# GpSimd's 31 convolution sums dealt anew over the projection chunks of a layer

## The chip, the cores and the metric
The kernel runs on one core of one Trainium2 chip. The metric is the device time of an execution in microseconds (us); the number compared is the median of the runs.

## The reference
A first block (pooling, sparse attention, convolutional feed-forward) is followed by a second block of two layers, in float32, for 512 tokens of width 1024. The change lies in the mixing layer of the second block, which both layers run:

```
u = h @ w_in
a_b, a_c, a_x, q, k, v, c_in = split(u)
y_a = a_b * causal_depthwise_conv(a_c * a_x, short_conv_w)          # 3 taps
o   = rmsnorm(diff_attention(rope(q), rope(k), v, lam)) * (1 - lam_init)   # 4 heads
c   = c_in + glu_b
c   = c[:, :256] * sigmoid(c[:, 256:])
c   = causal_depthwise_conv(c, conf_dw_w) + conf_dw_b               # 31 taps, 256 channels
y_c = silu(layernorm(c))
out = concat(y_a, o, y_c) @ w_out
```
The 31-tap convolution is `conv[t] = b + sum over k of w[k] * c[t - 30 + k]`, for each of 256 channels. They lie as two groups of 128 on the partitions.

## The kernel before
Activations are kept transposed, features on the partitions and the 512 tokens along the free axis. A product with weights runs through chunks. A chunk is eight 128x128 weight blocks (512 KB), 1024 input by 128 output features, and gives one 128x512 output tile (in a group of four chunks the blocks are dealt otherwise). To keep float32 accuracy with the faster float32r matmuls, every operand is split in a high part and a remainder: `wh` and `wl` for the weights, `xh` and `xl` for the activations. A chunk is 24 matmuls: per block `wh*xh` and `wh*xl` (16, L486 and L487, or L543, L544, L574, L575 in grouped chunks), then eight `wl*xh` (L506, L550, L582).

The chunks go through the engines like this:
- SyncE loads chunk t into one of four slots of `raw`. It waits until the remainder of chunk t-4 is done.
- ScalarE makes the high part: `head(t)`, a copy `wh <- raw` (L972, 128x1024). There are two slots, so head(t+2) waits until TensorE has finished chunk t.
- GpSimd makes the remainder: `rest(t)`, two subtractions `wl <- raw, wh` (L428), after head(t). Here it is called a pass.
- TensorE waits for `hi_ready` before the first matmul of a chunk and for `lo_ready` before the last eight.
- VectorE takes the result out of PSUM.

The projection of a layer of the second block has 22 chunks (n = 0 to 21). Chunks 0 to 3 compute the 31-tap convolution's input together (a group over four banks), 4 to 7 the values, 8 to 15 the queries and keys of four heads in turn, 16 to 21 the three-tap branch. The order on every engine is written out by hand. Beside chunk n each engine has two slots, s = 2n and 2n + 1. From slot 21 on the attention steps of head h occupy slots 21 + 4h to 31 + 4h: scores (TensorE, L892 and L894), maximum (VectorE, L1823), exponentials (ScalarE, L1229), scaling of the probabilities (VectorE, L1832 and L1328), transposes (TensorE, L904), the product with the values (TensorE, L911), and the norm.

The queries and keys need a rotation. When chunk n (8 to 15) is done, ScalarE copies the bank to `ybuf` (L972, `rope_in`) and then does head(n + 2). TensorE rotates it in the first slot of chunk n + 1 (L881), VectorE multiplies and adds (L1331 or L1900; L1789; L1793 writes `lq` or `lk`). The score of a head's first step waits for the rotated key.

The 31-tap convolution is dealt between the engines. VectorE does channel group 0: one fused multiply and add per tap (L1328, `conv <- cpad, par, conv`), 23 of them up to the first slot of chunk 10 and then one per chunk. Group 1 is done by two engines. ScalarE writes the product of tap k, `tprod <- cpad` (L972, in the function `products` of the scalar block), and GpSimd adds it: `tap(k)`, a drain (L446), a wait for the product (L447) and `conv <- conv, tprod` (L448); tap 0 is a multiply on GpSimd itself (L443). Two product buffers alternate, so the product of tap k waits for the sum of tap k - 2 (`tap_added`). Tap 0 and the products wait for `glu_out`, VectorE's signal that the convolution's input is there (L1813).

GpSimd's order before is: pass of chunk n, then from chunk 5 on some sums: three each in chunks 5 to 9 (15), two each in 10 to 17 (16). ScalarE's order within chunk n is, for each of the two slots: the attention steps, then products; at the end the wait for TensorE's chunk n, the ybuf copy, head(n + 2), and for n = 7 the four copies of the values. It makes 2 and 1 products in the two slots of chunks 5 to 9 and 1 and 1 after.

The sums' result is read for the layer norm in slot 38 (chunk 19).

Of the kernel before, what the change touches and what calls it, by code (L numbers as in the profile page):

```python
# [46 lines left out]
TAPS = 31  # L47
# [42 lines left out]


HEAD_SLOT = 21

Y_ORDER = ("head0", "head1", "ya0", "head2", "head3", "ya1", "conv0", "conv1")
NORM_OF_HEAD = (1, 2, 3, 5)
# [34 lines left out]
def layer_slots(n):  # L130

    for half in range(2):
        s = 2 * n + half
        yield s, [(h, s - HEAD_SLOT - 4 * h) for h in range(4) if 0 <= s - HEAD_SLOT - 4 * h <= 10]

# [7 lines left out]
def build(nc, x, positions, positions2, weights, par1, par2, consts, masks, w1, w2, pool_w, out):  # L143
    ctx = ExitStack()
    with ctx:
# [65 lines left out]
        def c2(name, i=0):  # L211
            return par[:, P2[name] + i:P2[name] + i + 1]
# [133 lines left out]
        def cols(start, n):  # L346
            return slice(start, start + n) if isinstance(start, int) else bass.ds(start, n)
# [71 lines left out]
        @block.gpsimd  # L419
        def _(pool):  # L420
            def rest(t):

                v = t.value()
                pool.wait_ge(hi_ready, (t + 1).value())
                half = CB * P // 2
                for h in range(2):
                    two = cols((v % 2) * (CB * P) + h * half, half)
                    x_ = pool.tensor_tensor(wl[:, :, :].rearrange("p s n -> p (s n)")[:, two],  # L428
                                            raw[:, cols((v % 4) * (CB * P) + h * half, half)],
                                            wh[:, :, :].rearrange("p s n -> p (s n)")[:, two].bitcast(F32),  # L430
                                            ALU.subtract)
                x_.then_inc(lo_ready, 1)

            with pool.Fori(0, T_BLOCK1) as t:
                rest(Count(0).loop(t, 1))

            with pool.Fori(0, LAYERS) as l:
                T = Count(T_BLOCK1).loop(l, T_LAYER)

                def tap(k):  # L440

                    if k == 0:
                        pool.tensor_scalar(conv[:, 1, :], cpad[:, 1, 0:S], c2("dw_w", TAPS), c2("dw_b", 1),  # L443
                                           ALU.mult, ALU.add)
                    else:
                        pool.drain()  # L446
                        pool.wait_ge(R["tap_prod"], Count(k).loop(l, TAPS - 1).value())  # L447
                        pool.tensor_tensor(conv[:, 1, :], conv[:, 1, :], tprod[:, k % 2, :], ALU.add)\  # L448
                            .then_inc(R["tap_added"], 1)

                done = 0
                for n in range(T_LIN):
                    if n == 5:
                        pool.wait_ge(R["glu_out"], Count(1).loop(l, 1).value())
                    rest(T + n)
                    if n >= 5:
                        upto = min(done + (3 if n < 10 else 2), TAPS)
                        for k in range(done, upto):
                            tap(k)
                        done = upto  # L460
                with pool.Fori(T_LIN, T_LAYER) as t:
                    rest(T.loop(t, 1))
            for t in range(T_ALL, T_ALL + 2):
                rest(Count(t))
# [505 lines left out]
        def _(act):  # L970
            def copy(o, i, scale=1.0):
                return act.activation(o, i, ACT.Copy, scale=scale)  # L972
# [140 lines left out]
            for p in range(NP):  # L1113
                j, k = p // 8, p % 8
                t, n = T_IN + 3 * j, N_IN + 4 * j
# [25 lines left out]
            for j in range(NT):  # L1141
                t, n = T_IN + 12 + 3 * j, N_IN + 16 + 4 * j
# [6 lines left out]
                for c in range(2):  # L1149
                    k = 2 * j + c  # L1150
# [3 lines left out]
            def out_and_ffn(t, n, u, feed0, gain, h0, first_block):  # L1154
                def next_head(c):
                    act.wait_ge(chunk_done, (t + (c + 1)).value())
                    head(t + (c + 2))

                for c in range(4):
                    next_head(c)  # L1160
                for m in range(KD):
                    if m >= 4:
                        next_head(m)
                    feed(m, feed0 + m, gain("ffn_g", m), n + m)
                t, n = t + T_OUT, n + KD
                for c in range(2):
                    next_head(c)
                root(u, NT, scale=1.0 / D)
                for c in range(2, 4):
                    next_head(c)  # L1170
                hidden(n, h0, 0, first_block)
                next_head(4)
                hidden(n + 2, h0 + 1, 1, first_block)
                next_head(5)
                hidden(n + 4, h0 + 2, 2, first_block)
                with act.Fori(3, KF) as r:
                    for c in range(2):
                        act.wait_ge(chunk_done, (t + (c + 1)).loop(r, 2).value())
                        head((t + (c + 2)).loop(r, 2))
                    hidden(n.loop(r, 2), h0.loop(r, 1), r, first_block)  # L1180
                return t + T_UP, n + T_UP
# [27 lines left out]
            t, n = out_and_ffn(Count(T_IN + T_MIX), Count(N_IN + N_MIX), Count(8), Count(KD), gain1, Count(0), True)  # L1209
# [3 lines left out]
            with act.Fori(0, LAYERS) as l:  # L1213
# [24 lines left out]
                def y_head(name, src):  # L1238
                    copy(yh[:, Y_ORDER.index(name), :], src).then_inc(R["y_hi"], 1)
# [27 lines left out]
                def products(n):  # L1267

                    for k in range(made[0], min(made[0] + n, TAPS)):
                        if k == 1:  # L1270
                            act.wait_ge(R["glu_out"], L1.value())
                        if k > 2:
                            act.wait_ge(R["tap_added"], Count(k - 2).loop(l, TAPS - 1).value())
                        copy(tprod[:, k % 2, :], cpad[:, 1, k:k + S], scale=c2("dw_w", TAPS + k))\
                            .then_inc(R["tap_prod"], 1)
                    made[0] += n

                for n in range(4, T_LIN):
                    for half, (s, steps) in enumerate(layer_slots(n)):
                        if s == 11:  # L1280
                            act.wait_ge(R["lam_psum"], L1.value())
                            act.activation(lame, TR[:, 0:2], ACT.Exp).then_inc(R["lam_exp"], 1)
                        if s == 38:
                            act.wait_ge(R["ya_ready"], Count(1).loop(l, 2).value())
                            y_head("ya0", ya[:, 0, :])
                        for h, step in steps:
                            head_step(h, step)
                        if n >= 5:
                            products(2 if n < 10 and half == 0 else 1)
                        if s == 38:  # L1290
                            root(U0 + NORM_LN[0], NT, scale=1.0 / 256, plain=True)
                        if s == 40:
                            act.wait_ge(R["ln_sub"], L1.value())
                            act.activation(sq[:, :, :], conv[:, :, :], ACT.Square).then_inc(R["ln_sq"], 1)
                        if s == 42:
                            root(U0 + NORM_LN[1], NT, scale=1.0 / 256, eps=LN_EPS)
                    act.wait_ge(chunk_done, (T + (n + 1)).value())
                    if 8 <= n < 16:
                        i, m = n - 8, n - 4
                        if i >= 2:  # L1300
                            act.wait_ge(rot_ready, Count(6 + i).loop(l, 8).value())
                        b = QK0[i] if i < 2 else G[(N + m).even()]
                        copy(ybuf[:, i % 2, :], b[:, :]).then_inc(R["rope_in"], 1)
                    head(T + (n + 2))
                    if n == 7:
                        act.wait_ge(recip_ready, (U0 + 1).value())
                        for i in range(NT):
                            copy(lv[:, :, i, :], VB[i][:, :].rearrange("p (h d) -> p h d", d=P),
                                 scale=s_recip[:, i:i + 1]).then_inc(R["v_out"], 1)
                act.wait_ge(R["ya_ready"], Count(2).loop(l, 2).value())  # L1310
                y_head("ya1", ya[:, 1, :])
                for c in range(2):
# [4 lines left out]
                t, n = out_and_ffn(T + T_LIN, N + N_LIN, U0 + 7, Count(3 * KD).loop(l, 2 * KD), gain2,  # L1317
                                   Count(KF).loop(l, KF), False)
# [776 lines left out]
```

## Time and profile before

| | |
|---|---|
| median of 3 runs | 1987.17 us (1985.21 to 1987.58) |
| profiled execution: time, span | 1989.08 us, 1987.3 us |
| TensorE busy, mean granted clock | 1918.2 us (97%), 0.987 |
| VectorE, ScalarE, GpSimd busy | 964.4, 735.3, 970.4 us |
| projection stage of layer 0, of layer 1 | 764 to 957, 1368 to 1559 us |

The profile comes from one execution; its times are measured from the start of the span. PE is TensorE, PEld its weight loads, DVE VectorE, ACT ScalarE, POOL GpSimd, and POOLq is GpSimd's sequencer (drains and waits). L446 is line 446 of the kernel. In a time line, what stands in brackets is how long the engine sat idle before the instruction and what released it. Matmuls overlap, so eight in a row take less than eight times one.

### The profile page before, as it was taken

Reading aid. Unit: us, or ns where it says so; the run is one execution under the profiler, and the core shown is the slowest. Engines: PE = TensorE matmul, PEld = TensorE weight load, DVE = VectorE, ACT = ScalarE, POOL = GpSimd, SP = SyncE. Lnnn points to the kernel's source line nnn. Section 1 sums busy time; section 2 is a strip of 40 time slices with the busy share of each in tenths; the row PEclk is TensorE's granted clock in tenths of the full one; section 3 lists DMA queues with packets and bytes.
Section 4 is the critical chain, followed back from the end, with each engine's and each line's share of the span. In section 5 each row is a group of like instructions: output and inputs, shape, how many; then the busy total and the mean of one; then the engine's idle time right before and its main releaser. Section 6 shows DMA issues by size and latency. Waiting matters only on the chain.

```text
span 1987.3 us, 28229 instructions
## 1 busy us (share of the span) xinstructions
PE 1918.2 (97%) x8670; PEld 1515.1 (76%) x8670; DVE 964.4 (49%) x1316; ACT 735.3 (37%) x1160; POOL 970.4 (49%) x692
## 2 busy tenths in 40 slices
PE   6999999999999999899999999999899999999996
PEld 5866668878888888667788888887666788888885
DVE  7667644456665122877443333221977443333213
ACT  4235553432223223455433322222555443332222
POOL 4322224446666454853444555454854345455553
PEclk9999999999999999999999999999999999999998
DMA  6111112222222322211232222232111222322232
GB/s 242 64 54 43 44 54 95 96 85 95 95 95 95 106 99 92 73 45 54 79 101 96 95 95 95 98 103 98 63 54 61 77 90 92 104 95 95 95 106 84
DMA packets 48952, 173.89 MB, mean 88 GB/s; under 512 B 5488, under 2 KB 6512, under 8 KB 48624
## 3 DMA queue, kind: packets, MB, share of 16 engines
q1 hardware_dynamic: 48880, 172.96, 25.8%
q8 instruction: 42, 0.69, 0.1%
q14 instruction: 30, 0.25, 0.0%
HBM read 169.82 MB, written 2.10 MB: 87 GB/s over the span
## 4 chain that ended last, share of the span: by engine, by line
PE 81%; DVE 6%; POOLq 3%; issue 3%; DVEq 2%; ACT 2%; POOL 1%; DMA 1%; ACTq 0%; SPq 0%
PE bank L506 21%; PE bank L486 20%; PE bank L487 20%; PE bank L543 3%; PE bank L550 3%; PE bank L544 3%; POOLq L446 3%; PE bank L520 1%; PE bank L744 1%; PE bank L526 1%; PE bank L521 1%; DVE lp L1832 1%; PE bank L773 1%; POOL wl L428 1%; PE bank L787 1%
## 5 line engine op out<-in xcount | busy, mean ns | idle before, releaser
L428 POOL TENSOR_TENSOR wl<-raw,wh (+1 forms) x626 | 883.6, 1433 | 921.7 <-ACT wh L972 907.9
L972 ACT ACTIVATE wh<-raw 128x1024 fp32r (+1 forms) x313 | 331.7, 1060 | 827.1 <-PE bank L506 694.4
L486 PE MATMUL bank<-xh,wh 128*128 128x512 f32 x1336 | 533.2, 399 | 5.5 <-DVE tmp L1371 5.5
L487 PE MATMUL bank<-xl,wh 128*128 128x512 f32 x1336 | 524.3, 392 | 0.0
L506 PE MATMUL bank<-xh,wl 128*128 128x512 f32 x1336 | 343.2, 396 | 3.4 <-POOL wl L428 3.4
L486 PEld LDWEIGHTS bank<-xh,wh 128*128 128x128 f32 x1336 | 253.7, 190 | 65.5 <-issue 7.9
L506 PEld LDWEIGHTS bank<-xh,wl 128*128 128x128 f32 x1336 | 249.6, 189 | 63.8 <-issue 7.1
L487 PEld LDWEIGHTS bank<-xl,wh 128*128 128x128 f32 x1336 | 253.5, 190 | 56.4 <-issue 3.8
L486 PE MATMUL bank<-hh,wh 128*128 128x512 f32 x528 | 208.0, 394 | 0.0
L487 PE MATMUL bank<-hl,wh 128*128 128x512 f32 x528 | 208.0, 394 | 0.0
L1371 DVE TENSOR_TENSOR ybuf<-bank,rstd 128x512 f32<-128x512 f32 x95 | 65.3, 688 | 227.2 <-PE bank L506 225.2
L1740 DVE TENSOR_TENSOR tmp<-tmp,ybuf 128x512 f32<-128x512 f32 x66 | 106.6, 1614 | 74.4 <-ACT tmp L1189 74.2
L1702 DVE TENSOR_TENSOR xs<-xs,bank 128x512 f32<-128x512 f32 (+1 forms) x48 | 32.1, 684 | 227.7 <-PE bank L506 179.3
L506 PE MATMUL bank<-hh,wl 128*128 128x512 f32 x528 | 134.8, 394 | 0.0
L448 POOL TENSOR_TENSOR conv<-conv,tprod 128x512 f32<-128x512 f32 x60 | 85.4, 1424 | 80.7 <-ACT tprod L972 72.6
L506 PEld LDWEIGHTS bank<-hh,wl 128*128 128x128 f32 x528 | 98.7, 187 | 24.5
L486 PEld LDWEIGHTS bank<-hh,wh 128*128 128x128 f32 x528 | 98.7, 187 | 24.4
L487 PEld LDWEIGHTS bank<-hl,wh 128*128 128x128 f32 x528 | 98.7, 187 | 24.4
L543 PE MATMUL bank<-xh,wh 128*128 128x512 f32 x192 | 76.8, 400 | 9.1 <-ACT wh L972 8.4
L972 ACT ACTIVATE hh<-tmp 128x512 f32 (+1 forms) x66 | 41.7, 632 | 117.1 <-DVE tmp L1740 117.1
L1328 DVE SCALAR_TENSOR_TENSOR conv<-cpad,par,conv 128x512 f32<-128x512 f32 x60 | 80.4, 1340 | 4.9
L1742 DVE TENSOR_TENSOR hl<-tmp,hh 128x512 f32 (+1 forms) x66 | 51.1, 774 | 59.8 <-ACT hh L972 59.8
(285 smaller groups left out, 2333.0 us busy)
## 6 DMA issues: line engine op xcount, KB each, us to landing
raw<-in_weights SPq DMA_DIRECT2D x313, 512.0 KB, 3.2
xs<-in_x SPq DMA_DIRECT2D x4, 512.0 KB, 6.9
out_t<-xs SPq DMA_DIRECT2D x8, 256.0 KB, 2.2
w1k<-in_w SPq DMA_DIRECT2D x1, 1024.0 KB, 9.6
w1v<-in_w SPq DMA_DIRECT2D x1, 1024.0 KB, 11.1
shifted<-kvraw SPq DMA_DIRECT2D x8, 124.0 KB, 2.4
posi<-in_positions SPq DMA_DIRECT2D x2, 256.0 KB, 8.8
cst<-in_consts SPq DMA_DIRECT2D x1, 290.0 KB, 5.4
```

Of the source, the lines that this page charges most:

```text
L428: x_ = pool.tensor_tensor(wl[:, :, :].rearrange("p s n -> p (s n)")[:, two], raw[:, cols((v % 4) * (CB * P) + h * half, half)], wh[:, :, : ...
L446: pool.drain()
L448: pool.tensor_tensor(conv[:, 1, :], conv[:, 1, :], tprod[:, k % 2, :], ALU.add)\
L486: mm(b[:, :], w, kh(k), start=first and k == 0, stop=False)
L487: mm(b[:, :], w, kl(k), start=False, stop=False)
L506: i = mm(b[:, :], wl[:, s, (blk0 + k) * P:(blk0 + k + 1) * P], kh(k), start=False, stop=last and k == blocks - 1)
L543: mm(X4[a][:, :], w, kh(k), start=k == 0, stop=False)
L544: mm(X4[a][:, :], w, kl(k), start=False, stop=False)
L972: return act.activation(o, i, ACT.Copy, scale=scale)
L1328: return stt(out=o, in0=a, scalar=s, in1=b, op0=ALU.mult, op1=ALU.add)
L1371: return tt(o, b[:, :], rstd[:, :], ALU.mult).then_inc(tile_out, 1)
L1740: tt(tmp[:, 1, :], tmp[:, 0, :], ybuf[:, 0, :], ALU.mult).then_inc(R["prod_ready"], 1)
```

## The change
GpSimd's sums follow a table: none in chunk 5, three in 6, two in 7, four in each of 8 to 13, two in 14. The wait for `glu_out` on GpSimd moves from ahead of pass 5 to ahead of pass 6. ScalarE's products follow the same table, one chunk ahead: in each of the two slots of chunk n it makes half (rounded down) of the sums that GpSimd has in chunk n + 1. Those are 1 and 1 in chunks 5 and 6, 2 and 2 in 7 to 12, 1 and 1 in 13, none after. Operations, data and their number are the same.

```diff
--- before.py
+++ after.py
@@ -90,6 +90,8 @@
 
 
 HEAD_SLOT = 21
+
+POOL_TAPS = {6: 3, 7: 2, 8: 4, 9: 4, 10: 4, 11: 4, 12: 4, 13: 4, 14: 2}
 
 Y_ORDER = ("head0", "head1", "ya0", "head2", "head3", "ya1", "conv0", "conv1")
 NORM_OF_HEAD = (1, 2, 3, 5)
@@ -450,14 +452,13 @@
 
                 done = 0
                 for n in range(T_LIN):
-                    if n == 5:
+                    if n == 6:
                         pool.wait_ge(R["glu_out"], Count(1).loop(l, 1).value())
                     rest(T + n)
-                    if n >= 5:
-                        upto = min(done + (3 if n < 10 else 2), TAPS)
-                        for k in range(done, upto):
-                            tap(k)
-                        done = upto
+                    for k in range(done, done + POOL_TAPS.get(n, 0)):
+                        tap(k)
+                    done += POOL_TAPS.get(n, 0)
+                assert done == TAPS
                 with pool.Fori(T_LIN, T_LAYER) as t:
                     rest(T.loop(t, 1))
             for t in range(T_ALL, T_ALL + 2):
@@ -1285,8 +1286,7 @@
                             y_head("ya0", ya[:, 0, :])
                         for h, step in steps:
                             head_step(h, step)
-                        if n >= 5:
-                            products(2 if n < 10 and half == 0 else 1)
+                        products(POOL_TAPS.get(n + 1, 0) // 2 if n >= 5 else 0)
                         if s == 38:
                             root(U0 + NORM_LN[0], NT, scale=1.0 / 256, plain=True)
                         if s == 40:
```

## Rows read from the trace of the kernel before
**Rows 1.** The page's first part: busy us, share, instructions of each engine.
```profile
PE 1918.2 (97%) x8670; PEld 1515.1 (76%) x8670; DVE 964.4 (49%) x1316; ACT 735.3 (37%) x1160; POOL 970.4 (49%) x692
```
**Rows 2.** The chain of waits, 800 to 836 us: shares of the stretch by line.
```profile
by line: POOLq L446 70.8%; POOL wl L428 22.1%; issue 8.1%; POOL conv L448 1.5%; POOLq L447 1.1%; POOLq L428 0.6%; POOLq L424 0.4%
```
**Rows 3.** Time line of GpSimd: start, us, engine, line, operation, out<-in, [idle before <-releaser].
```profile
792.62 2.74 POOL L428 TENSOR_TENSOR wl<-raw,wh 128x512 fp32r<-128x512 f32 x2 [6.80 <-DVE cpad L1813]
799.90 3.41 POOL L428 TENSOR_TENSOR wl<-raw,wh 128x512 fp32r<-128x512 f32 x2
...
819.69 1.47 POOL L448 TENSOR_TENSOR conv<-conv,tprod 128x512 f32<-128x512 f32 x1 [0.23 <-issue]
821.39 1.48 POOL L448 TENSOR_TENSOR conv<-conv,tprod 128x512 f32<-128x512 f32 x1 [0.23 <-issue]
...
832.99 3.43 POOL L428 TENSOR_TENSOR wl<-raw,wh 128x512 fp32r<-128x512 f32 x2
...
851.68 1.28 POOL L448 TENSOR_TENSOR conv<-conv,tprod 128x512 f32<-128x512 f32 x1 [2.71 <-ACT tprod L972]
```
**Rows 4.** Waits of TensorE, 760 to 1000 us: us in total, times, longest.
```profile
PE bank L892 <- DVE lk L1793: 5.0, 3, 2.3
PE bank L582 <- POOL wl L428: 4.3, 2, 2.8
PE bank L506 <- POOL wl L428: 1.6, 2, 0.8
PE bank L881 <- ACT ybuf L972: 1.0, 2, 0.8
```
**Rows 5.** Time line of TensorE, layer 0.
```profile
811.98 3.78 PE L582 MATMUL bank<-wl,xh 128*128 128x512 f32 x8 [2.83 <-POOL wl L428]
...
820.42 1.98 PE L506 MATMUL bank<-xh,wl 128*128 128x512 f32 x8
...
837.51 0.29 PE L892 MATMUL bank<-msk 128*128 128x128 bf16 x2
```
**Rows 6.** Windows: length, busy us (count) of PE, PEld, DVE, ACT, POOL; PEclk; DMA; GB/s.
```profile
799.90:836.65 36.75, 30.07 (x111) 22.00 (x110) 35.09 (x27) 16.32 (x24) 33.49 (x24) 0.91 0.17 58
810.00:820.00 10.00, 8.02 (x23) 6.34 (x24) 9.63 (x7) 5.39 (x8) 9.10 (x8) 0.66 0.15 52
880.00:890.00 10.00, 8.54 (x36) 6.20 (x37) 7.59 (x15) 5.47 (x14) 6.18 (x4) 0.83 0.16 54
```
**Rows 7.** Time line of ScalarE, layer 0: head, product, rotation copies.
```profile
792.89 1.06 ACT L972 ACTIVATE wh<-raw 128x1024 fp32r x1 [1.39 <-PE bank L582]
...
822.90 0.73 ACT L972 ACTIVATE tprod<-cpad,par 128x512 f32<-128x512 f32 x1 [0.98 <-POOL conv L448]
823.53 0.58 ACT L972 ACTIVATE ybuf<-bank 128x512 f32<-128x512 f32 x1
...
832.02 0.58 ACT L972 ACTIVATE ybuf<-bank 128x512 f32<-128x512 f32 x1
...
839.89 0.59 ACT L972 ACTIVATE ybuf<-bank 128x512 f32<-128x512 f32 x1
...
885.98 0.59 ACT L972 ACTIVATE ybuf<-bank 128x512 f32<-128x512 f32 x1
```
**Rows 8.** Time line of VectorE, layer 0.
```profile
818.30 6.80 DVE L1328 SCALAR_TENSOR_TENSOR conv<-cpad,par,conv 128x512 f32<-128x512 f32 x4
...
835.98 0.99 DVE L1793 TENSOR_TENSOR lk<-tmp,tmp 128x512 f32<-128x512 f32 x1
...
882.82 1.61 DVE L1328 SCALAR_TENSOR_TENSOR lp<-lp,small 128x512 f32<-128x512 f32 x1
...
930.40 0.75 DVE L1328 SCALAR_TENSOR_TENSOR lp<-lp,small 128x512 f32<-128x512 f32 x1
```
**Rows 9.** Time line of ScalarE, layer 1: head 6 and chunk 10's copy.
```profile
1396.65 1.07 ACT L972 ACTIVATE wh<-raw 128x1024 fp32r x1 [1.39 <-PE bank L582]
...
1443.51 0.59 ACT L972 ACTIVATE ybuf<-bank 128x512 f32<-128x512 f32 x1
```

## The prediction
> **What bounds the kernel now.** I began with the page. TensorE is busy 97% of the span [rows 1], so only stretches in which it waits or runs slowly can be won, and only new ones can be lost. GpSimd is at 49%, but that is an average. In the two layers' projection stages the chain of waits is different: from 800 to 836 us, 70.8% of it is GpSimd's drain (L446) and 22.1% the remainder pass (L428) [rows 2]. So I went through the engines' time lines there. "Chunk n" is projection chunk n (0 to 21) of layer 0; ACT is ScalarE, DVE is VectorE.
>
> GpSimd does one remainder pass per chunk, then its sums. Pass 6 starts at 799.90, pass 7 at 808.55 and pass 10 at 832.99: (832.99 - 799.90)/4 = 8.27 us per chunk of one pass and three sums. Sums follow each other every 1.70 us (819.69, 821.39). So a pass with its gaps is 8.27 - 5.10 = 3.17 us [rows 3]. TensorE needs less for a chunk (24 matmuls, eight of them in 1.98 us [rows 5]), and waits for passes 6, 7, 9 and 10, 4.3 + 1.6 = 5.9 us in four waits [rows 4]. After the longest, 2.83 us, its granted clock is 0.66 over 810 to 820 [rows 6]: between 1.2 and 2.4 GHz that is 6.8 us at the lower level, 3.4 us of work lost (eight matmuls take 3.78 us there [rows 5]). That is about 9 us per layer on TensorE's side.
>
> ACT is tied to the same chain. Product k waits for sum k-2 (two buffers). At the end of chunk n, behind that chunk's products in ACT's order, come the copy of the rotation input (ybuf) and head n+2. The ybuf copy of chunk 8 starts at 823.53, 0.63 us after a product that had waited 0.98 us for GpSimd; that of chunk 9 at 832.02, that of chunk 10 at 839.89 [rows 7]. TensorE's rotation waits up to 0.8 us for them [rows 4].
>
> DVE has no slack either: 35.09 us busy of 36.75 from 799.90 to 836.65, its own sums at 1.70 us, in step with GpSimd's (four in 6.80) [rows 6, 8]. It finishes the first rotated key at 835.98 + 0.99 = 836.97 [rows 8]; TensorE takes it at 837.51 [rows 5]. So whatever happens to the remainder waits, the first score cannot come over 0.5 us earlier unless DVE is faster, and it does the same operations beside a GpSimd that is still busy.
>
> **The change part by part.**
>
> *Wait for glu_out one pass later.* Pass 5 no longer waits 6.80 us [rows 3]. It moves from 792.62 to about 789. TensorE waited only for the four passes above, so this gains nothing there; it only takes one pass out of the queue behind the wait. GpSimd's chain now begins with pass 6, which needs head 6: ACT ends that at 792.89 + 1.06 = 793.95 [rows 7]. The old chain began at 792.62.
>
> *Sums and products.* Before, sums per GpSimd chunk: 3 in chunks 5 to 9, 2 in 10 to 17. After: 3 in 6, 2 in 7, 4 in 8 to 13, 2 in 14. ACT's products by chunk were 3 in 5 to 9, then 2; now 2 in 5 and 6, 4 in 7 to 12, 2 in 13. The last product of ACT's chunk n used to need the second sum (chunks 10 up: the first) of GpSimd's chunk n. Now, in chunks 7 to 12, it needs the second sum of GpSimd's chunk **n+1**, behind pass n+1. Behind it on ACT stand ybuf and head n+2, for which TensorE, DVE and GpSimd wait.
>
> I follow GpSimd with the measured pieces. The first cycle (pass and sums 0 to 2) takes 799.90 - 792.62 = 7.28. Then a pass is 3.17 and a sum 1.70.
> Pass 7 starts at 793.95 + 7.28 = 801.2; pass 8 at + 6.57 (two sums) = 807.8; pass 9 at + 9.97 (four sums) = 817.8; pass 10 at 827.7; pass 11 at 837.7.
> The second sum of a chunk ends 3.17 + 3.40 = 6.57 after its pass starts: sum 6 at 814.4, sum 10 at 824.3, sum 14 at 834.3, sum 18 at 844.3.
> A product's 0.63 us later ybuf starts: at 825.0 for chunk 8 (before 823.53, +1.5), 835.0 for chunk 9 (before 832.02, +3.0), 844.9 for chunk 10 (before 839.89, +5.0).
> GpSimd has no gap in this: a product is there 0.7 us after the sum two before it, and a head ends 1.6 us after the start of the ybuf copy ahead of it (0.58 and 1.06): head 10 at 826.6 for the pass at 827.7, head 11 at 836.6 for 837.7.
>
> The last piece is uncertain: DVE's dense sums end near 836, and beyond that a sum takes 1.28 (at 851.68) instead of 1.47 (at 819.69) [rows 3]. Passes took between 2.74 and 3.43 [rows 3]; I take 0.4 less there. That makes +5.0 into +4.2. I take +4.7 for a layer at the chunk-10 copy. TensorE's four remainder waits go, but it waits instead for head 9 and for the copies of chunks 8 and 9 (some 6 to 8 us for the first: it would arrive near 818), so the 9 us do not come back. Such a wait is longer than the one that was followed by the lower clock; that slow stretch would end before the next copy, so I add nothing.
>
> Layer 1 repeats this: from head 6 to the copy of chunk 10 it has 1443.51 - 1396.65 = 46.86 us [rows 9], layer 0 has 47.00. So +9.4 us for the early term.
>
> The Trainium skill ("SBUF — State Buffer", section "Who interferes with whom") says that a VectorE operation with two SBUF inputs and a GpSimd operation that reads SBUF exclude each other for the whole instruction. Taken strictly, a pair would cost 1.28 + 0.75 = 2.03 us, and the cycle of four sums 11.3 us, which would put the chunk-10 copy another 6 us later in each layer (18 sums at 0.33). The trace has 1.70 for a pair [rows 3, 8], so the slowing is there but not the full exclusion; the sum above goes by 1.70.
>
> *After chunk 10.* Here GpSimd keeps up (four sums and a pass in 9.97 against (885.98 - 839.89)/4 = 11.5 us for a chunk [rows 7]), and the chain runs through DVE, ACT and TensorE: the score maximum, the exponentials, the product, ybuf, then DVE's multiply of it and the scaling of the probabilities. In either kernel 13 or 14 of GpSimd's sums are left for this part. Differences:
> - ACT: one more product between exponentials and ybuf in chunks 11 and 12, +0.63 each by [rows 7]; one less in 14, 15 and 16, -0.63 each.
> - DVE: the same operation on the probabilities takes 1.61 beside GpSimd and 0.75 alone [rows 8]. The sums are denser in chunks 11 to 13 and gone in 15 to 17. A second sum right behind the first in chunks 10 to 12 falls on DVE's scaling of the probabilities: two operations of that kind, up to +1.7 a chunk. From 14 on about 0.9, one such, comes back a chunk.
> - What can come back on TensorE: its three waits for the rotated keys, 5.0 us in all, 2.3 the longest [rows 4], and slow clock behind them (0.83 over 880 to 890 [rows 6]: 1.7 us of work).
>
> Bounds for this term in a layer: -7 (5.0 + 1.7, all of it goes) and +6 (three chunks at +1.7, two products at 0.63). I take 0, since the same number of sums meets the same chain. Both layers: -14 to +12.
>
> The end of the sums (chunk 14 instead of 17) is worth nothing by itself: the layer norm that needs them is in slot 38 (chunk 19).
>
> **Sum.** Early +9.4 (8.4 to 10.2), late 0 (-14 to +12): the profiled execution, 1989.08 us (span 1987.3 and 1.8 around it), becomes 1998.5. It lay 1.9 above the median 1987.17; against that median the forecast is 1996.6.
>
> **The rivals.**
> 1. *Slower by contention too* (chance 0.2): the late term near its upper end, where GpSimd's second sum keeps falling on DVE's scaling and slow stretches follow longer waits. 1987.2 + 9.4 + 9 = 2006. For it: 1.61 against 0.75. Against: GpSimd idles more from chunk 15 on.
> 2. *Made good later* (0.15): TensorE's waits in chunks 14 to 16 are shorter by what the products and sums no longer take, 4 to 5 us a layer, 9 in all. 1987.2 + 9.4 - 9 = 1988: no change.
> 3. *Faster* (0.15), the other side: the copies of chunks 8 to 10 turn out not to hold TensorE, because GpSimd's pieces are quicker once its order is less tight, and the remainder waits with their slow clock (9 us a layer) are gained. Its point of decision is whether sum 10 ends before about 821 (instead of 824.3), and DVE must speed up too. At half its worth, 1987.2 - 9 = 1978. Against it: DVE's 836.97.
> 4. The forecast (0.5): 1997, own range 1992 to 2002.
>
> That the sums would not move at all is excluded by the code.
>
> **How the numbers follow.** Two in ten outside leaves 1984 to 2009. The measurement can tell about 0.2% (4 us) from no change. Faster takes 0.15 of rival 3; same takes rival 2 (0.15) and a little of the forecast's lower tail, 0.17; slower is the rest, 0.68.
>
> **What would show it.** In the changed trace: no wait of TensorE for L428 in the stage; four sums per pass from pass 8 on, cycles near 10 us; ybuf copies of chunks 8, 9, 10 at +1.5, +3.0, +5 against head 6; TensorE waiting for ybuf some 7 us in chunk 9; the step from ybuf of chunk 10 to the stage's end as long as before. It would be wrong if cycles of four sums are well under 9.5, if products don't stand ahead of ybuf in time, or if chunks 14 to 16 give back more than 5 us a layer.

## The result and the profile after

The changed kernel takes 1998.14 us (median of 5, 1996.99 to 2000.13) against 1987.17 (5 runs, 1985.21 to 1989.90): ratio 1.0057, 95% interval 1.0046 to 1.0068. It is 11 us slower; forecast were 10 (1997). The profiled execution of the changed kernel took 1996.99 us with a span of 1995.2, 7.9 more than the span before; before's profiled execution lay 1.9 above its median and this one 1.2 below its own, so the trace shows 3 us less than the medians.

In the changed kernel every line below the new table has moved by one or two (L428 is L430, L446 is L448, L486 is L487, L972 is L973). Stage times are easier to compare from a common start, so I take the start of head 6 on ScalarE: 792.89 before, 792.37 after.

The chain of waits after, 800 to 836 us, answers to [rows 2]:

```profile
by line: POOLq L448 69.8%; POOL wl L430 17.5%; issue 9.0%; POOL conv L450 3.0%; POOLq L449 1.2%; POOLq L430 0.6%; POOLq L426 0.4%
```
GpSimd still paces this stretch. Its time line after (start, us, engine, line, operation; compare [rows 3]), passes 8 to 12, and sums 17 and 18 behind pass 11:

```profile
807.71 3.44 POOL L430 TENSOR_TENSOR wl<-raw,wh 128x512 fp32r<-128x512 f32 x2
...
817.88 2.50 POOL L430 TENSOR_TENSOR wl<-raw,wh 128x512 fp32r<-128x512 f32 x2
...
827.04 3.41 POOL L430 TENSOR_TENSOR wl<-raw,wh 128x512 fp32r<-128x512 f32 x2
...
836.99 3.43 POOL L430 TENSOR_TENSOR wl<-raw,wh 128x512 fp32r<-128x512 f32 x2
840.65 1.29 POOL L450 TENSOR_TENSOR conv<-conv,tprod 128x512 f32<-128x512 f32 x1 [0.23 <-issue]
842.16 1.29 POOL L450 TENSOR_TENSOR conv<-conv,tprod 128x512 f32<-128x512 f32 x1 [0.23 <-issue]
...
846.38 2.58 POOL L430 TENSOR_TENSOR wl<-raw,wh 128x512 fp32r<-128x512 f32 x2
```
The cycles with four sums take 10.17, 9.16, 9.95 and 9.39 us (9.97 was forecast). ScalarE after, against [rows 7]: head 6, the copies of chunks 8 and 9, and chunk 10's last product and copy.

```profile
792.37 1.06 ACT L973 ACTIVATE wh<-raw 128x1024 fp32r x1 [1.39 <-PE bank L583]
...
824.38 0.58 ACT L973 ACTIVATE ybuf<-bank 128x512 f32<-128x512 f32 x1
...
834.51 0.58 ACT L973 ACTIVATE ybuf<-bank 128x512 f32<-128x512 f32 x1
...
843.48 0.72 ACT L973 ACTIVATE tprod<-cpad,par 128x512 f32<-128x512 f32 x1 [0.79 <-POOL conv L450]
844.11 0.58 ACT L973 ACTIVATE ybuf<-bank 128x512 f32<-128x512 f32 x1
```
The copy of chunk 10 follows a product that waited for GpSimd's sum 18 (842.16 + 1.29), which itself stands behind pass 11. Before, that copy waited for nothing on GpSimd. After head 6 the three copies come at 32.0, 42.1 and 51.7 us, before at 30.6, 39.1 and 47.0: +1.4, +3.0 and +4.7.

TensorE's waits after, 760 to 1000 us (us in total, times, longest), against [rows 4]:

```profile
PE bank L882 <- ACT ybuf L973: 7.8, 4, 5.7
PE bank L893 <- DVE lk L1793: 5.1, 4, 2.8
PE bank L487 <- ACT wh L973: 2.2, 1, 2.2
```
No wait for a remainder pass (L430) is left. In their place TensorE waits 2.17 us for head 9, up to 816.29, and 5.70 us for chunk 8's copy, up to 825.09. The granted clock in that stretch (columns as in [rows 6]):

```profile
810.00:820.00 10.00, 7.22 (x27) 5.03 (x25) 9.55 (x8) 5.92 (x9) 9.11 (x7) 0.86 0.17 52
820.00:830.00 10.00, 4.91 (x10) 3.21 (x11) 9.53 (x8) 4.21 (x6) 9.11 (x7) 0.50 0.16 52
```
The granted clock is 0.50 for the whole slice from 820, the lower of its two levels. It had fallen at about 817, one microsecond after the wait of 2.17 us and before the long one, and it rose again at 830.6. TensorE still waits 0.81 us for the next copy (L882 at 835.22), so that slow stretch cost nothing.

The first rotated key and the first score come later too:

```profile
835.12 0.69 DVE L1900 TENSOR_TENSOR tmp<-bank,tmp 128x512 f32<-128x512 f32 x1 [0.72 <-ACT ybuf L973]
...
838.28 1.01 DVE L1793 TENSOR_TENSOR lk<-tmp,tmp 128x512 f32<-128x512 f32 x1
```
VectorE waits for chunk 9's late copy, and the key is ready 46.9 us after head 6, before 44.1 [rows 8].

From the copy of chunk 10 to ScalarE's first copy of the convolution's result (`yh <- conv`, the end of the stage) layer 0 takes 120.5 us, before 121.5; layer 1 takes 120.5, before 120.3. In between the distance to before grows to +8.5 at chunk 13's copy and shrinks again, to +3.7 at the end of layer 0's stage.

### The profile page after: what moved, and what is told of

It reads as the page before. It is cut to its first block, busy times and chain, and to the rows that moved or that the text cites. A ratio compares the mean times of both kernels' runs of the same rounds, so it can differ in the third digit from the quotient of the medians.

```text
span 1995.2 us, 28229 instructions
## 1 busy us (share of the span) xinstructions
PE 1916.3 (96%) x8670; PEld 1513.3 (76%) x8670; DVE 965.6 (48%) x1316; ACT 736.7 (37%) x1160; POOL 962.4 (48%) x692
## 4 chain that ended last, share of the span: by engine, by line
PE 82%; DVE 6%; POOLq 3%; DVEq 2%; ACT 2%; issue 2%; POOL 1%; DMA 0%; ACTq 0%; SPq 0%
PE bank L507 21%; PE bank L487 20%; PE bank L488 20%; POOLq L448 3%; PE bank L551 3%; PE bank L544 3%; PE bank L545 3%; PE bank L521 1%; PE bank L527 1%; PE bank L745 1%; PE bank L522 1%; PE bank L912 1%; PE bank L774 1%; POOL wl L430 1%; DVE lp L1832 1%
## 5 line engine op out<-in xcount | busy, mean ns | idle before, releaser
L430 POOL TENSOR_TENSOR wl<-raw,wh (+1 forms) x626 | 877.0, 1423 | 979.6 <-ACT wh L973 979.4
L973 ACT ACTIVATE wh<-raw 128x1024 fp32r (+1 forms) x313 | 331.7, 1060 | 833.1 <-PE bank L507 694.1
L487 PE MATMUL bank<-xh,wh 128*128 128x512 f32 x1336 | 535.8, 401 | 9.8 <-DVE tmp L1371 5.5
L507 PE MATMUL bank<-xh,wl 128*128 128x512 f32 x1336 | 341.7, 395 | 0.0
L487 PEld LDWEIGHTS bank<-xh,wh 128*128 128x128 f32 x1336 | 254.7, 191 | 71.2 <-ACT wh L973 10.0
L507 PEld LDWEIGHTS bank<-xh,wl 128*128 128x128 f32 x1336 | 249.6, 189 | 58.4 <-issue 6.7
L487 PE MATMUL bank<-hh,wh 128*128 128x512 f32 x528 | 208.0, 394 | 0.0
L507 PE MATMUL bank<-hh,wl 128*128 128x512 f32 x528 | 134.8, 394 | 0.0
L507 PEld LDWEIGHTS bank<-hh,wl 128*128 128x128 f32 x528 | 98.7, 187 | 24.5
L487 PEld LDWEIGHTS bank<-hh,wh 128*128 128x128 f32 x528 | 98.7, 187 | 24.5
L973 ACT ACTIVATE hh<-tmp 128x512 f32 (+1 forms) x66 | 41.7, 632 | 117.0 <-DVE tmp L1740 117.0
L1328 DVE SCALAR_TENSOR_TENSOR conv<-cpad,par,conv 128x512 f32<-128x512 f32 x60 | 81.9, 1365 | 4.9
L1742 DVE TENSOR_TENSOR hl<-tmp,hh 128x512 f32 (+1 forms) x66 | 51.1, 774 | 59.8 <-ACT hh L973 59.8
## 6 DMA issues: line engine op xcount, KB each, us to landing
w1v<-in_w SPq DMA_DIRECT2D x1, 1024.0 KB, 10.7
```

Source lines behind the costliest of these rows:

```text
L487: mm(b[:, :], w, kh(k), start=first and k == 0, stop=False)
L507: i = mm(b[:, :], wl[:, s, (blk0 + k) * P:(blk0 + k + 1) * P], kh(k), start=False, stop=last and k == blocks - 1)
L1328: return stt(out=o, in0=a, scalar=s, in1=b, op0=ALU.mult, op1=ALU.add)
```

## The experiments

All are runs of the whole kernel. This table is worked out from ScalarE's time lines: us after head 6 in layer 0, and in the last two columns the stretch from chunk 10's copy to `yh <- conv`, layer 0 / layer 1, and the median change in time against the runs of the kernel before on the same chip.

| kernel | copy 8 | copy 9 | copy 10 | copy 11 | copy 13 | copy 15 | after copy 10 | time, us |
|---|---|---|---|---|---|---|---|---|
| before | 30.6 | 39.1 | 47.0 | 58.6 | 80.4 | 105.9 | 121.5 / 120.3 | 0 |
| changed | 32.0 | 42.1 | 51.7 | 64.1 | 88.9 | 111.8 | 120.5 / 120.5 | +11.0 |
| same-chunk products | 24.7 | 34.7 | 46.5 | 59.0 | 84.4 | 109.0 | 123.0 / 125.3 | +6.2 |
| three ahead | 32.9 | 41.9 | 49.1 | 59.8 | 82.9 | 109.1 | 124.4 / 121.0 | +8.8 |
| dense early only | 32.0 | 42.1 | 49.4 | 59.8 | 81.9 | 106.8 | 119.7 / 119.2 | +4.2 |
| dense late only | 30.6 | 39.1 | 51.4 | 63.7 | 88.4 | 111.3 | 120.4 / 120.4 | +11.8 |
| sums, no products | 21.8 | 29.5 | 45.9 | 56.9 | 80.7 | 103.5 | 119.3 / 119.3 | -3.4 |
| products, no sums | 22.3 | 28.1 | 37.9 | 48.1 | 71.0 | 93.9 | 117.7 / 116.4 | -24.1 |
| neither | 21.8 | 28.1 | 36.0 | 45.1 | 65.8 | 88.6 | 113.0 / 113.0 | -35.4 |
| late products | 32.0 | 42.1 | 49.4 | 61.1 | 85.3 | 109.3 | 120.3 / 119.2 | +5.8 |
| more early | 29.5 | 39.7 | 50.8 | 61.7 | 85.5 | 109.6 | 119.1 / 119.5 | +5.1 |
| vector relief | 25.1 | 33.6 | 43.1 | 55.2 | 80.4 | 104.7 | 128.7 / 129.7 | +11.0 |
| vector only | 30.6 | 39.1 | 46.3 | 58.0 | 79.7 | 105.2 | 125.2 / 123.7 | +8.1 |
| tap slot | 30.7 | 39.2 | 46.0 | 56.3 | 77.2 | 101.4 | 116.2 / 116.3 | -9.8 |

**Where the 11 us arise.** The first four runs split the change in two ways: products one chunk ahead or not, and early or late half.

Same-chunk products: the table of sums as changed.

```diff
-                        products(POOL_TAPS.get(n + 1, 0) // 2 if n >= 5 else 0)
+                        products(POOL_TAPS.get(n, 0) // 2)
```


> The changed kernel's table of sums (four per cycle in chunks 8 to 13), but ScalarE makes the products in the same chunk as the sums, as before, not one chunk ahead. Coupling theory (the last product of a chunk must not hang on GpSimd's next chunk, behind which the ybuf copy and the next head stand): the copies of chunks 8 and 9 are not held by GpSimd any more, the copy of chunk 10 comes 47 to 48 us after head 6 (before 47.0, changed 51.7), the first score stays where VectorE's rotated key allows it, and the time is 1987 to 1991. Volume theory (a cycle of a pass and four sums, about 10 us, is too long by itself, whoever waits): copy of chunk 10 stays near 51, time 1996 to 2000, with TensorE waiting for passes 9 and 10 instead.

1993.66 us (10 runs) against 1987.43, ratio 1.0029 (1.0019 to 1.0039). The copies do what the coupling theory said, chunk 10's is 0.5 us earlier than before, and TensorE waits for passes instead:

```profile
PE bank L507 <- POOL wl L430: 6.6, 4, 2.3
```
The time lies between the two expectations. The coupling before chunk 10 goes away, but the later stretch is 1.5 and 5.0 us longer (123.0 and 125.3). That four products and their sums in one chunk cause this was not tested. The first score comes 43.0 us after head 6, 1.6 sooner than before: GpSimd stands idle 2.30 us for the first product there, and VectorE's first 13 multiply-adds take 20.00 us instead of 21.56.

Three ahead: the old numbers, one GpSimd chunk later.

```diff
-POOL_TAPS = {6: 3, 7: 2, 8: 4, 9: 4, 10: 4, 11: 4, 12: 4, 13: 4, 14: 2}
+POOL_TAPS = {**{n: 3 for n in range(6, 11)}, **{n: 2 for n in range(11, 19)}}
...
-                        products(POOL_TAPS.get(n + 1, 0) // 2 if n >= 5 else 0)
+                        if n >= 5:
+                            products(2 if n < 10 and half == 0 else 1)
```


> Three sums per cycle in chunks 6 to 10, then two in 11 to 18: the old numbers, one GpSimd chunk later, so that ScalarE's products keep the old schedule and are one chunk ahead; the wait for glu_out is one pass later as in the change. It has the coupling without the volume. Both theories that need the volume: copies of chunks 8, 9 and 10 at +1.4, +1.3 and 0 against before (sum 10 ends at 793.95 + 7.28 + 2 x 8.27 + 6.57 = 824.4), time 1987 to 1990. If coupling alone were enough: the copy of chunk 10 at +4 or more and 1995 or more.

1996.20 us, ratio 1.0043 (1.0029 to 1.0057): a miss. The time is that of the second reading, the copy (+2.1) that of neither. Head 7 already comes 1.5 us later, since product 3 in chunk 5 now waits for sum 1 behind pass 6. So the lag of GpSimd by one chunk costs also with three sums. The stretch behind copy 10 is 2.9 and 0.7 us longer. In layer 0 it takes 12.1 us from head 18 to head 19, where the granted clock is 0.75 (915 to 925), in layer 1 9.3 us at 1.00; why it falls there is open.

Dense early only:

```diff
-POOL_TAPS = {6: 3, 7: 2, 8: 4, 9: 4, 10: 4, 11: 4, 12: 4, 13: 4, 14: 2}
+POOL_TAPS = {6: 3, 7: 2, 8: 4, 9: 4, 10: 4, **{n: 2 for n in range(11, 18)}}
```


> The changed kernel up to chunk 10 (3, 2, 4, 4, 4 sums), then two per chunk in 11 to 17; products one chunk ahead. It takes the dense part of chunks 11 to 13 away. If the early delay is the whole cost and the later part only trades (the changed trace shows +8.5 us at chunk 13's copy against before and +3.7 at the end): the copies of chunks 11 to 13 stay near +5 instead of +5.5, +7.6 and +8.5, nothing is given back in 14 to 17, time 1996 to 2000. If the dense part costs by itself: 1990 to 1994.

1991.63 us (11 runs), ratio 1.0024 (1.0015 to 1.0033). Chunks 8 and 9 are exactly as late as in the changed kernel, and the first key too (46.9 us after head 6). But chunk 10's copy is 2.3 us earlier than there, 2.4 later than before. It now follows the exponentials and a product that waits for nothing. So the late first two copies pass on 2.4 us of their 3.0 to chunk 10; chunk 11's copy is still 1.2 later than before. The time falls under the second reading (1990 to 1994), but what is gone with the dense part is also the four products of chunk 10; the next two runs tell these apart.

Dense late only, the kernel before up to chunk 10:

```diff
-                        upto = min(done + (3 if n < 10 else 2), TAPS)
+                        upto = min(done + (3 if n < 10 else 4 if 11 <= n < 14 else 2), TAPS)
...
-                            products(2 if n < 10 and half == 0 else 1)
+                            products(2 if n < 10 and half == 0 or 10 <= n < 13 or n == 13 and half == 0 else 1)
```


> The kernel before up to chunk 10 (three sums in 5 to 9, two in 10), then four per chunk in 11 to 13 and two in 14, with two products per slot in chunks 10 to 12. It is the late half of the change alone. If the late part only trades: about +3 to +4 us at the copy of chunk 13, given back by chunk 17, time 1985 to 1988. If the dense sums beside the softmax chain cost by themselves: 1990 or more.

1999.18 us, ratio 1.0056 (1.0043 to 1.0070): the whole loss of the change, with the old chunks 8 and 9 and the first key at the old 44.1 us. The time falls under the second reading ("1990 or more"), but not for its reason: the loss is made in chunk 10, before the dense sums meet the softmax chain. ScalarE's time line there:

```profile
845.57 0.72 ACT L972 ACTIVATE tprod<-cpad,par 128x512 f32<-128x512 f32 x1 [3.24 <-POOL conv L448]
846.20 0.58 ACT L972 ACTIVATE ybuf<-bank 128x512 f32<-128x512 f32 x1
```
Four products in chunk 10 (16 to 19) make the copy wait for sum 17, which stands behind pass 11. From the copy on it takes 120.4 us in either layer (before 121.5 and 120.3).

The test of that is to take two of chunk 10's products out and make them later. Late products, the sums as in the changed kernel:

```diff
-                        products(POOL_TAPS.get(n + 1, 0) // 2 if n >= 5 else 0)
+                        if n >= 5:
+                            products({5: 1, 6: 1, 10: 1, 13: 2 - half, 14: 1 - half, **{i: 2 for i in (7, 8, 9, 11, 12)}}.get(n, 0))
```


> The changed kernel's table of sums as it is. Only the products of ScalarE change: two instead of four in chunk 10, then four in 11 and 12, three in 13 and one in 14, so that chunk 10's copy hangs on sum 16 (GpSimd's chunk 10) and not on sum 18 (its chunk 11). If the four products of chunk 10 are the place where the time is lost: copy of chunk 10 at 49.4 instead of 51.7 us after head 6, 2 to 3 us less per layer to the end, time 1991 to 1994. If the dense sums of chunks 11 to 13 are the cost: the bump moves to chunk 13 and the time stays 1996 to 1999.

1993.07 us (9 runs), ratio 1.0027 (1.0017 to 1.0037): 5 us less than the changed kernel, as the first reading said. Its product no longer waits:

```profile
843.14 0.72 ACT L973 ACTIVATE tprod<-cpad,par 128x512 f32<-128x512 f32 x1
843.75 0.59 ACT L973 ACTIVATE ybuf<-bank 128x512 f32<-128x512 f32 x1
```
(head 6 is at 794.40 here, so the copy is at 49.4). It did leave the dense sums of chunks 11 to 13 alone, and the copy of chunk 13 is 3.6 us earlier than in the changed kernel. The other half of the loss stays: the first key is as late as in the changed kernel (46.9), copy 10 is at +2.4, and the time is 5.8 us above before.

**What the sums and products cost at all.** Three kernels leave work out.

Sums, no products:

```diff
-                        pool.wait_ge(R["tap_prod"], Count(k).loop(l, TAPS - 1).value())
-                        pool.tensor_tensor(conv[:, 1, :], conv[:, 1, :], tprod[:, k % 2, :], ALU.add)\
+                        pool.tensor_tensor(conv[:, 1, :], conv[:, 1, :], cpad[:, 1, k:k + S], ALU.add)\
...
-                        products(POOL_TAPS.get(n + 1, 0) // 2 if n >= 5 else 0)
```


> The changed kernel's table of sums, but ScalarE makes no products and GpSimd adds the shifted input itself (the multiplication with the tap weights is left out of channel group 1, so its convolution is not the reference's). GpSimd's load and its meeting with VectorE stay; the products and every wait between ScalarE and GpSimd for them go. If the delay of chunk 10's copy (51.7 us after head 6) comes from ScalarE standing in wait for sum 18: it drops to 47 or less and the time to 1987 to 1991. If it comes from VectorE and GpSimd meeting: it stays near 50, time 1994 or more.

1983.90 us (10 runs), ratio 0.9984 (0.9975 to 0.9994). VectorE and TensorE there, the first rotated key and the first score:

```profile
836.13 0.81 DVE L1791 TENSOR_TENSOR lk<-tmp,tmp 128x512 f32<-128x512 f32 x1
```
```profile
837.00 0.28 PE L892 MATMUL bank<-msk 128*128 128x128 bf16 x2 [1.01 <-DVE lk L1791]
```
The copy of chunk 10 (45.9) is where the first reading put it, the time 3 us below its range. ScalarE is free, chunk 9's copy comes 12.6 us sooner than in the changed kernel, and the key is ready 836.94 - 793.02 = 43.9 us after head 6. Before it was 836.97 - 792.89 = 44.1 [rows 7, 8]. VectorE beside a busy GpSimd is the second bound, as forecast: the first score waits for the key alone and comes only 0.6 us sooner than before. The bound is not fixed: in the same-chunk run it lies 1.6 us lower.

Products, no sums, and neither (tap 0 alone is left on GpSimd, and nobody waits for sums). The first has the first part of this diff, the second both:

```diff
...
-                        pool.tensor_tensor(conv[:, 1, :], conv[:, 1, :], tprod[:, k % 2, :], ALU.add)\
-                            .then_inc(R["tap_added"], 1)
...
-                        products(POOL_TAPS.get(n + 1, 0) // 2 if n >= 5 else 0)
```


> The changed kernel's products on ScalarE, but GpSimd makes no sums after tap 0 and nobody waits for them (channel group 1 of the convolution is left out). It prices ScalarE's 30 products alone: 0.63 us each where one stands between exponentials and copy. Against the run without both: some 1 to 2 us a layer, 1 to 4 in all. VectorE alone is faster (0.75 instead of 1.70 per tap), so the first score comes well before 44.6 us after head 6: time 1960 to 1975.

> Neither products nor sums of channel group 1 (only tap 0; the rest of that convolution is left out). It is the floor that every dealing of the sums is measured against. If what the sums cost is mostly VectorE meeting GpSimd, it is within 2 to 4 us of the run with products alone and 1958 to 1972; if the products are what costs, it is 8 us or more below that run.

1963.16 and 1951.92 us (4 runs each), ratios 0.9874 (0.9859 to 0.9889) and 0.9821 (0.9806 to 0.9836). The products alone cost 11.2 us, more than the 1 to 4 expected. The second of the two readings for "neither" came true, 8 us or more below the run with products. The sums alone cost 1983.9 - 1951.9 = 32.0. Both by themselves would make 43.2; the changed kernel pays 46.2 and the kernel before 35.4. VectorE's own taps where GpSimd makes no sums:

```profile
796.46 15.49 DVE L1322 SCALAR_TENSOR_TENSOR conv<-cpad,par,conv 128x512 f32<-128x512 f32 x13
```
(from "neither"). 13 in 15.49 us, 1.19 each against 1.70 in [rows 8]. Over the 22 multiply-adds ahead of the first key that would be 11 us. The key is ready 10.1 us earlier than before, and the copy of chunk 10 comes 11.0 us earlier (36.0 against 47.0), with the products 9.1.

**Better dealings?** More early:

```diff
-POOL_TAPS = {6: 3, 7: 2, 8: 4, 9: 4, 10: 4, 11: 4, 12: 4, 13: 4, 14: 2}
+POOL_TAPS = {6: 4, 7: 4, 8: 4, 9: 4, 10: 3, 11: 2, 12: 2, 13: 2, 14: 2, 15: 2, 16: 1, 17: 1}
...
+                        products((POOL_TAPS.get(n, 0) - (n == 6) + 1 - half) // 2)
```


> Sums 4, 4, 4, 4, 3 in chunks 6 to 10, then 2 in 11 to 15 and 1 in 16 and 17; products in the same chunk as the sums. Nineteen sums instead of seventeen lie ahead of chunk 11, and no copy hangs on a later pass. The runs so far say: time is twice (copy of chunk 10 after head 6, plus about 120 us). If VectorE sets the first score, the copy comes at 46 to 47.5 as in the same-chunk run, and two sums fewer behind it save about 1 us a layer: 1985 to 1988. If more sums ahead of the first score delay it (pass 10 ends later), 1990 or more.

1992.53 us (10 runs), ratio 1.0026 (1.0017 to 1.0036). The second reading came true: TensorE waits 7.9 us for passes (L507) in layer 0 and the first score is late, 47.5 us after head 6 against 44.6, though the key is ready at 44.4. Copy 10 is at 50.8, in layer 1 at 49.1. The stretch behind is 2.4 and 0.8 us shorter than before.

Vector relief and vector only move two of VectorE's taps from chunk 9 to 17 and 18; the first also deals the sums 3 (chunks 6 to 12) and 2 (13 to 17), products in the same chunk.

```diff
-                TAP_PLAN = {4: (0, 2), 5: (2, 2), 6: (2, 2), 7: (2, 2), 8: (2, 2), 9: (2, 2)}
+                TAP_PLAN = {4: (0, 2), 5: (2, 2), 6: (2, 2), 7: (2, 2), 8: (2, 2), 9: (1, 1), 17: (1, 1), 18: (1, 1)}
```


> Three sums in chunks 6 to 12, two in 13 to 17, products in the same chunk, and VectorE moves two of its own taps from chunk 9 to chunks 17 and 18. If VectorE's dense taps (1.70 us each) set the first score, its rotated key is ready 3.4 us sooner, GpSimd's pass 10 (about 829 instead of 836) does not hold it, and chunk 10's copy comes at about 43.5 instead of 47: behind it two GpSimd sums and two products more (1 to 2 us): 1982 to 1986, faster than before. If VectorE is not the bound there: 1987 to 1991.

> The kernel before with only VectorE's two taps moved from chunk 9 to 17 and 18. If GpSimd's chain (pass 10 ends at 836.4) binds the first score as closely as VectorE does (836.97), this gains next to nothing there: 1986 to 1989, TensorE's waits for GpSimd unchanged. If VectorE alone binds it: 1981 to 1984.

1998.36 (ratio 1.0053, 1.0039 to 1.0067) and 1995.53 us (1.0046, 1.0032 to 1.0059). Both times miss both of their readings. Half of the expectation held: chunk 10's copy is 3.9 and 0.7 us sooner, 43.1 against 43.5 expected. The other half failed: taps in chunks 17 and 18 run into slot 38, where TensorE needs the finished convolution. In "vector only", layer 0:

```profile
933.28 2.85 PE L591 MATMUL bank<-cst,conv 128*128 128x1 f32 x16 [1.13 <-DVE conv L1328]
```
The wait itself is 1.1 us. Around it the granted clock is 0.70 (930 to 940; before 0.83), and from head 20 to head 21 it takes 15.1 us instead of 12.1. The stretch after copy 10 grows by 3.4 to 3.7 us in "vector only" and by 7.2 and 9.4 in "vector relief", where more sums are left for it as well. A tap's place counts, and that led to the last run. Tap slot, GpSimd and ScalarE as before:

```diff
-                TAP_PLAN = {4: (0, 2), 5: (2, 2), 6: (2, 2), 7: (2, 2), 8: (2, 2), 9: (2, 2)}
+                TAP_PLAN = {4: (0, 2), 5: (2, 2), 6: (2, 2), 7: (2, 2), 8: (2, 2), 9: (1, 1),
+                            12: (0, 2), 14: (0, 2), 18: (1, 0), **{n: (0, 1) for n in (10, 11, 13, 15, 16, 17)}}
```


> The kernel before, GpSimd and ScalarE unchanged. From chunk 10 on VectorE's own tap stands in the second slot of a chunk instead of the first, where VectorE would otherwise idle 1.8 to 1.9 us for the ybuf copy; in the first slot it stands ahead of the rotated key that TensorE waits for (conv at 879.20, then L1789, lk at 880.64, waits of 5.0 us in three). Two taps move from chunk 9 to the second slots of chunks 12 and 14. If VectorE's place on the softmax chain is what TensorE waits for: about 0.67 us a chunk from 10 to 15, 2 to 4 us a layer, first score 0.7 us sooner as in the run with two taps moved, time 1979 to 1984, faster than both kernels. If the idle time for ybuf merely moves (the copy comes as late as before): 1986 to 1989.

1978.12 us (5 runs, 1977.35 to 1979.55), ratio 0.9951 (0.9938 to 0.9965): 10 us faster than before, 20 faster than the changed kernel and a little better than expected. TensorE's waits for the rotated keys, 5.0 us in [rows 4], are:

```profile
PE bank L892 <- DVE lk L1793: 0.6, 2, 0.3
```
In the first slot the reduction is now followed at once by the key; the tap stands in the second slot, before the copy that VectorE waits for:

```profile
868.55 0.75 DVE L1328 SCALAR_TENSOR_TENSOR conv<-cpad,par,conv 128x512 f32<-128x512 f32 x1
870.39 0.69 DVE L1901 TENSOR_TENSOR tmp<-bank,tmp 128x512 f32<-128x512 f32 x1 [1.09 <-ACT ybuf L972]
...
874.32 1.28 DVE L1823 TENSOR_REDUCE small<-bank 128x1 f32<-128x512 f32 x2
875.51 0.68 DVE L1789 TENSOR_TENSOR tmp<-bank,tmp 128x512 f32<-128x512 f32 x1
876.28 0.69 DVE L1793 TENSOR_TENSOR lk<-tmp,tmp 128x512 f32<-128x512 f32 x1
```
How much of the 10 us belongs to the slots and how much to the two taps taken out of chunk 9 was not tried apart; copy 10 shows 1.0 us a layer for the second, the stretch behind it 4 to 5 us.

## Why the prediction was right, and where it was not

- *GpSimd's cycles and ScalarE's copies.* Held. The cycles are 9.7 us in the mean. Passes 8 to 11 start 0.1 to 0.6 us from the forecast once the 0.5 us earlier head 6 is allowed for, the copies at +1.4, +3.0, +4.7 (forecast +1.5, +3.0, +5, taken as +4.7).
- *No gain from the remainder waits.* Held: all are gone, and TensorE waits 2.2 us for head 9 and 5.7 for the copy (6 to 8 forecast). The slow stretch was absorbed, as said, though the prediction had it begin behind the long wait and it began before.
- *VectorE's 836.97 as a floor.* Held for the first score of a VectorE beside a steadily busy GpSimd, shown by the sums without products (43.9 against 44.1 us). Its condition, "unless DVE is faster", matters: the same-chunk run had the key at 43.0.
- *The early term, +4.7 a layer.* The size was right, and so was what sets chunk 10's copy: its last product waits for sum 18 (ends 843.45), behind pass 11. What the prediction did not see is that two ways lead to this copy. One goes from chunk 9's late copy over the first key to the exponentials and makes +2.4; it is all that is left in "dense early only" and "late products". The other is the product of chunk 10 that waits for a sum behind pass 11. By itself it makes +4.4, in "dense late only", with copies 8 and 9 on time. The longer one counts, so their lateness does not add up. Taking the second way out ("late products") gives back 5 of the 11 us. The loss of 5.8 us that is left comes with +2.4 a layer at copy 10.
- *The late term taken as 0.* Held: -1.0 and +0.2 us. But its bounds were -7 and +6, and that two larger things cancel so closely is in part luck: the distance grows from +4.7 to +8.5 at chunk 13 and goes back to +3.7. How much of the growth is products and how much contention was not taken apart. Part of layer 0's -1.0 is a slow stretch that before had in slots 37 to 39 of layer 0 alone (heads 20 to 21 take 12.1 us there and 10.8 in layer 1; the granted clock is 0.83 over 930 to 940).
- *The rivals.* "Made good later" needed the late stretch to shrink by over 4 us a layer; it did not. "Slower by contention too" needed it to grow; it did not either. "Faster" needed sum 10 to end before about 821; it ended at 823.72. The exclusive use that the Trainium skill states ("SBUF — State Buffer", section "Who interferes with whom") would have put a sum and a VectorE tap at an estimated 2.03 us a pair (1.28 + 0.75). The measurement decides against it: the sums of the changed kernel still follow each other in about 1.69 us while VectorE's taps run, and 1.50 later. Its direction, that the two slow each other, is borne out by 1.19 against 1.70 us per tap.

"Same-chunk products" takes 2.4 us more behind chunk 10 in layer 1 than in layer 0. Of this 1.4 us lie between heads 20 and 21 (12.1 against 10.7 us), where the granted clock is 0.83 in layer 1 (1538 to 1548) and 1.00 in layer 0; what makes it fall in one layer alone is not settled. Not settled either is what the products' 11.2 us consist of beyond their place before the copies.

## What to carry to other kernels

When two engines pass work through a two-deep buffer, look at what else stands behind the producer's wait on its own queue: running one step ahead makes the producer wait for the consumer's next step, and everything queued behind the producer with it. Where two late things meet in front of the same instruction, only the later one counts: mending one of them gives back the difference and not its own length. Before dealing filler work by count, find the places where the engine idles on the chain: moving VectorE's tap from in front of the key to the idle time before a copy, together with two taps out of the dense chunk 9, gave 10 us, and no new dealing of GpSimd's sums gave anything.

## What the runs showed of the hardware

- A VectorE multiply-add over 128x512 with all operands in SBUF takes 1.70 us from start to start, a drain included, beside a GpSimd that is always busy. Beside one that makes only its passes and the first tap ("neither", GpSimd busy 8.9 of 15.5 us) it takes 1.19 us in the mean, and 0.81 where GpSimd is nearly idle (four in 3.23 us at 814.45). GpSimd's sum takes 1.47 us beside VectorE's dense taps and 1.28 behind them.
- The price of work off the bottleneck was large: without the other, 60 sums on GpSimd cost 32 us of the whole kernel, 60 products on ScalarE 11 us, although both engines are under half busy (49% and 37% before).
- In the changed kernel TensorE waited 2.17 us, worked about one, and then had the lower granted clock (0.50) from 817 to 830.6, over the wait of 5.70 us and the 5.5 us of work behind it. Matmuls took 0.63 us instead of 0.39. This cost nothing, since the next wait was for the same chain.
